# Four gate projections of z brought forward into the first four rounds of a chunked delta rule

## The reference

```
h = rms_norm(x);  proj = h @ w_in      # glu_a glu_b q k v z a b gate_a gate_b
c = silu(layer_norm(conv31(glu_a * sigmoid(glu_b))));  y_conv = c @ w_conv_out
q, k, v = silu(conv5(q, k, v)); q, k normed per head (8 heads of 128)
o = delta_rule(q, k, v, g, beta) + reversed delta_rule   # chunks along the sequence
o = rms_norm(o) * silu(z);             y_delta = o @ w_delta_out
x = x + (sigmoid(gate_a) * y_conv + sigmoid(gate_b) * y_delta) @ w_o
```

## Time and profile before

| | |
|---|---|
| median of three runs | 2165.98 us (2165.07 to 2167.03) |
| profiled execution, its time | 2168.76 us |
| profiled execution, its span | 2167.0 us |
| mean granted TensorE clock | 0.995 |
| PE, DVE, ACT, POOL busy | 2105.1, 1210.3, 853.3, 154.5 us |
| rounds 0 to 3 | 216.2 to 412.3 us of the span |
| rounds 4 to 7 | 499.1 to 696.0 us |

### The profile page before, as it was taken

How to read it: one execution, slowest core, us unless ns; L and a number is a source line. 1 busy time by engine, 2 the same in 40 slices (tenths; PEclk the granted TensorE clock), 3 DMA queues, 4 the chain that set the end, 5 groups by cost and what they waited for, 6 DMA issues and landing times.

```text
span 2167.0 us, 35176 instructions
## 1 busy us (share of the span) xinstructions
PE 2105.1 (97%) x14346; PEld 1747.7 (81%) x14346; DVE 1210.3 (56%) x1888; ACT 853.3 (39%) x1400; POOL 154.5 (7%) x134
## 2 busy tenths in 40 slices
PE   6999999999999999999999999999999999999998
PEld 5878777787878888888888888888897688888887
DVE  4789888798645554444433644443247835444323
ACT  4344655346674333333223533332243544322222
POOL 0100021002421010000000100000000110000000
PEclk9999999999999999999999999999999999999999
DMA  4242111122012342233323233233212122333321
GB/s 166 81 134 80 60 46 50 60 78 65 31 63 87 127 159 88 97 97 97 120 94 107 69 90 96 96 101 111 98 59 62 37 69 79 96 96 97 116 94 53
DMA packets 56173, 189.95 MB, mean 88 GB/s; under 512 B 6256, under 2 KB 8688, under 8 KB 56048
## 3 DMA queue, kind: packets, MB, share of 16 engines
q1 hardware_dynamic: 53168, 182.92, 26.4%
q10 hardware_dynamic: 2880, 5.24, 0.6%
HBM read 178.70 MB, written 9.44 MB: 87 GB/s over the span
## 4 chain that ended last, share of the span: by engine, by line
PE 65%; DVE 3%; ACT 1%; issue 0%; POOL 0%; DVEq 0%; ACTq 0%
PE pg L716 61%; PE pC L820 1%; DVE w_lo L2021 1%; PE pA L794 0%; PE pC L794 0%; PE pB L778 0%; ACT w_hi L1393 0%; PE pB L747 0%; DVE a_lo L2080 0%; DVE sml L2680 0%; DVE sm L2678 0%; PE pA L754 0%; DVE mo L2717 0%; PE pC L1308 0%; ACT a_hi L1953 0%
## 5 line engine op out<-in xcount | busy, mean ns | idle before, releaser
L716 PE MATMUL pg<-a_hi,w_hi 128*128 128x512 f32 (+1 forms) x1920 | 747.4, 389 | 14.2 <-ACT ptile L1483 4.4
L716 PE MATMUL pg<-a_lo,w_hi 128*128 128x512 f32 (+1 forms) x1920 | 739.9, 385 | 0.0
L716 PE MATMUL pg<-a_hi,w_lo 128*128 128x512 f32 (+1 forms) x1920 | 737.9, 384 | 0.0
L2021 DVE TENSOR_TENSOR w_lo<-w_raw,w_hi 128x1024 fp32r<-128x1024 f32 (+3 forms) x299 | 386.3, 1292 | 386.7 <-ACT w_hi L1393 386.0
L1393 ACT ACTIVATE w_hi<-w_raw 128x1024 fp32r<-128x1024 f32 (+3 forms) x299 | 329.6, 1102 | 646.0 <-PE pg L716 635.4
L716 PEld LDWEIGHTS pg<-a_hi,w_hi 128*128 128x128 f32 x1920 | 362.3, 189 | 91.3 <-issue 9.2
L716 PEld LDWEIGHTS pg<-a_hi,w_lo 128*128 128x128 f32 x1920 | 361.9, 188 | 68.9 <-issue 1.4
L716 PEld LDWEIGHTS pg<-a_lo,w_hi 128*128 128x128 f32 x1920 | 362.3, 189 | 67.8 <-issue 0.9
L716 PE MATMUL pg<-h_hi,w_hi 128*128 128x512 f32 (+1 forms) x572 | 213.5, 373 | 0.5 <-DVE w_lo L2021 0.5
L716 PE MATMUL pg<-h_hi,w_lo 128*128 128x512 f32 (+1 forms) x572 | 213.3, 373 | 0.0
L716 PE MATMUL pg<-h_lo,w_hi 128*128 128x512 f32 (+1 forms) x572 | 213.2, 373 | 0.0
(11 more groups left out here) (397 smaller groups left out, 2216.7 us busy)
## 6 DMA issues: line engine op xcount, KB each, us to landing
w_raw<-in_w_gu SPq DMA_DIRECT2D x132, 512.0 KB, 3.5
w_raw<-in_w_in SPq DMA_DIRECT2D x74, 512.0 KB, 3.5
w_raw<-in_w_dn SPq DMA_DIRECT2D x48, 704.0 KB, 4.1
spill_g<-tmp ACTq DMA_DIRECT2D x16, 256.0 KB, 2.2
w_raw<-in_w_co SPq DMA_DIRECT2D x8, 512.0 KB, 3.9
w_raw<-in_w_do SPq DMA_DIRECT2D x8, 512.0 KB, 3.7
w_raw<-in_w_wo SPq DMA_DIRECT2D x8, 512.0 KB, 4.2
w_raw<-in_w_pg SPq DMA_DIRECT2D x8, 512.0 KB, 3.5
```

What stands on the lines that cost most here:

```text
L716: ins = pe.matmul(dst[:, cols], w_of(w, n % 2, k), b(k)[:, cols], start=first and q == 0, stop=last and q == len(todo) - 1)
L2021: dve.tensor_tensor(w_lo[:, n % 2, 0:c], w_raw[:, n % 4, 0:c], w_hi[:, n % 2, 0:c].bitcast(F32), ALU.subtract).then_inc(S("w_lo"), 1)
```

## The change

Rounds 0 to 3 get a fourth filler, z4 to z7. Round 4 keeps gates 14 and 15, round 5 gets z0 and z1, round 6 gets z2 and z3; these three now have two fillers each and are dealt out by a new list `GAP2`. Round 7 keeps its four. The order of units and banks follows. Rounds 0 to 3 now use `GAP` and get 12 taps instead of 10 at gap 14; round 4 gets 16 taps instead of 24. Some waits for spills are counted anew, and SP waits for `on_z` before it loads the first two gates back.

```diff
+        FILLERS = [[("gate", 3 * R + 1), ("gate", 3 * R + 2), ("gate", 3 * R + 3), ("z", HH + R)] for R in range(4)] + [
+            [("gate", 14), ("gate", 15)], [("z", 0), ("z", 1)], [("z", 2), ("z", 3)], [("co", f) for f in range(4)]]
...
         GAP = [16, 17, 4, A_, B_, A_, B_, 1, B_] + [A_, B_] * 2 + [6, 8, 8]
-        GAP3 = [14, 14, 2, 3, 3, 3, 3, 1, 3] + [3, 3] * 2 + [4, 5, 5]
-        TAP = [1, 2, 0] + [1, 2] * 2 + [1, 3, 1, 2, 1, 3] + [0, 10, 0]
-        TAP4 = [1, 2, 0] + [1, 1] * 4 + [1, 2] + [0, 10, 0]
+        GAP2 = [9, 9, 4, 2, 2, 2, 2, 1, 2, 2, 2, 2, 2, 2, 2, 3]
+        TAP = [1, 2, 0] + [1, 2] * 2 + [1, 3, 1, 2, 1, 3] + [0, 12, 0]
+        TAP4 = [1, 1, 0] + [1, 1] * 5 + [0, 4, 0]
...
-        FILLERS = [[("gate", 3 * R + f) for f in range(1, 4)] for R in range(4)] + [
-            [("gate", 14), ("gate", 15), ("z", 0)], [("z", f) for f in range(1, 4)],
-            [("z", f) for f in range(4, 8)], [("co", f) for f in range(4)]]
...
-            gaps = GAP3 if len(filler(R)) == 3 else GAP
+            gaps = {2: GAP2, 4: GAP}[len(filler(R))]
...
                         if t < 2:
                             sp.wait_ge(S(f"spill{t}"), 16 * 10)
+                            sp.wait_ge(S("on_z"), 3 + t)
...
-                elif k in (13, 14):
+                elif k in (17, 18):
                     act.wait_ge(S("ons"), HH)
-                elif k < 18:
+                elif k < 22:
                     act.wait_ge(S(f"spill{k % 2}"), 16 * (k // 2))
-                elif k < 22:
-                    act.wait_ge(S("on_z"), k - 17)
                 else:
-                    act.wait_ge(S(f"spill{k % 2}"), 16 * (k // 2 - 2))
+                    act.wait_ge(S("on_z"), k - 21)
```

More of the change, by code:

```diff
@@ L323, in qkv_units, with filler_units @@
                     U.add(("qkv", 3 * h + i), a["w_in"][(2 + i) * KT + h], KT * P)
+        FILLERS = [[("gate", 3 * R + 1), ("gate", 3 * R + 2), ("gate", 3 * R + 3), ("z", HH + R)] for R in range(4)] + [
+            [("gate", 14), ("gate", 15)], [("z", 0), ("z", 1)], [("z", 2), ("z", 3)], [("co", f) for f in range(4)]]
+        TAIL = (("gate", 0), ("gate", 13))
+        def filler_units(half):
+            for key in [TAIL[half]] + sum(FILLERS[NC * half:NC * half + 4 - half], []):
+                U.add(key, a["w_in"][{"gate": 6, "z": 5}[key[0]] * KT + key[1]], KT * P)
         qkv_units(0)
-        for i in range(13):
-            U.add(("gate", i), a["w_in"][6 * KT + i], KT * P)
+        filler_units(0)
         qkv_units(1)
[L329 to L332, removed]
+        filler_units(1)
         for nm in ("co", "do", "wo"):
@@ L380, in build @@
         O.add(("ab",), "D")
-        TAIL = (("gate", 0), ("gate", 13))
         def qkv_outs(half):
@@ L389, in qkv_outs @@
             O.add(TAIL[half], "A")
[L391 to L398, removed]
+        for half in range(2):
+            qkv_outs(half)
+            for key in sum(FILLERS[NC * half:NC * half + 4 - half], []):
+                O.add(key, "A")
         for i in range(8):
@@ L484, in build @@
         UNIT = 3 * KT
-        assert sum(GAP) == 4 * UNIT and sum(GAP3) == 3 * UNIT and \
+        assert sum(GAP) == 4 * UNIT and sum(GAP2) == 2 * UNIT and \
             4 * GLU_TAPS[0] + 6 * GLU_TAPS[1] + sum(sum(z) for q in QKV_TAPS for z in q) + 4 * sum(TAP) + sum(TAP4) >= len(TAPS)
@@ L1583, in head_squares @@
                         if g < 2:
-                            act.wait_ge(S(f"spill{g}"), 16 * (7 - g))
+                            act.wait_ge(S(f"spill{g}"), 16 * (9 - g))
                         else:
```

## The result

The changed kernel takes 2187.18 us (median of 3, 2185.73 to 2187.54) against 2165.98, and the ratio on record is 1.0085 with a 95% interval of 1.0071 to 1.0099. By these medians it is slower by 21 us (a quotient of 1.0098), where I had said 8. The ratio fits about 2168.5 us for the kernel before, and that is also the mean of its 91 executions further down; by it the loss is 18 us. The profiled execution took 2185.73 us. Lines in a row are those of the kernel it comes from: 984, 1002, 1039, 1112, 1129 and 1718 of the changed kernel are 989, 1007, 1044, 1117, 1134 and 1725 before, and 1002, 1020, 1130, 1147 and 1737 in the version with two units moved are 989, 1007, 1117, 1134 and 1725 before.

What follows compares the result with a forecast made beforehand. PE was taken as dense nearly throughout, with DVE setting the pace in rounds 0 to 3. Terms +7.3 and -4.7 gave +2.6, plus +5 for clock falls: 2176.4 us profiled, about 2174 median, range 2161 to 2183.

Steps and rivals of the forecast that it cites:

- Round 0, +6.4: Round 0 with a fourth filler: 2.7 us stall for yb in level 3 and a longer DVE-set tail, +6.4 us.
- Rounds 1 to 3, +2.8, -0.6, -1.3: Fourth filler partly hidden; rounds 2 and 3 each regain 3.4 us as their old clock falls go.
- The table load that the last silu brings: End of rounds 0 to 2: one more ACT table load, 1.28 us, hidden in 2 us of slack.
- Rounds 4 to 6, structure -4.7: Rounds with two fillers, tied by ACT or POOL steps: +0.6, +0.5 and -5.8 us, sum -4.7.
- the term of the clock: Emptier rounds 4 to 6, and round 0: two to three clock falls of 2 to 3 us each, +5 us.
- B: Clock stays low through rounds 4 to 6, over half of about 140 us: 12 to 15 us, about 2183; chance 0.12.
- A: Fillers of rounds 0 to 3 hide in ub waits, falls go, rounds 5 and 6 shrink: about 2159 us; chance 0.15.
- C: No new clock falls, the two old ones go, only structure counts: 2169 us; chance 0.23.
- D: The old clock falls stay in rounds 2 and 3 as well: 2180 us; chance 0.08.
- The taps: Round 0 to 3 tails: 12 taps of about 0.67 us, 8.0 us, before oT; round 4 has eight taps less.

Runs made afterwards that it cites:

- the version with two units moved: Against the kernel before, only two units of z moved, to rounds 2 and 3 (fillers 3, 3, 4, 4, 3, 3, 2), taps as before: ratio 1.0009.
- the version with 24 products ahead: Against the changed kernel, rounds with two fillers put 24 instead of 18 products ahead of the levels: 2173.88 us, ratio 1.0025 to the kernel before.
- the run with filled waits: Changed kernel plus 63 products of no use in nine PE waits of rounds 0, 4, 5 and 6: 2178.40 us, ratio 1.0046 to the kernel before.
- the version with two moved and the gate output behind `yb`: Two units moved, with round 6's gate table and gate output put behind yb and kt of level 2: ratio 1.0006 to the kernel before.

## Why the prediction was wrong

**Round 0, +6.4: right.** Measured +7.7 with one fall in it. Line 1002 of level 3 waits for `yb` by 2.15 us (2.7 forecast). The tail, from line 1112 to the next round, is 14.2 us long (254.97 to 269.20), as forecast, and the two rows of DVE above show its cause: `w_lo`, the taps and `oT` set its end. What the forecast lacks lies ahead of line 1112 and is the fall: from level 0 to there the round takes 25.4 us (229.56 to 254.97), and 23.9 (229.72 to 253.66) in the version with 24 products ahead, whose round 0 has the same instructions and a clock of 1.00:

```profile
213.90:267.90 54.00, 47.68 (x736) 37.71 (x735) 44.85 (x85) 34.00 (x67) 4.56 (x7) 1.00 0.23 73
```

**Rounds 1 to 3, +2.8, -0.6, -1.3: right,** +2.6, -0.6 and -1.6. Both old falls are gone, and the waits at line 1112 with them, 0.2 us in rounds 1 and 2. The table load that the last silu brings cost nothing, as forecast: no wait at the head of these rounds is for ACT.

```profile
PE pC L1002 <- ACT yb L1718: 1.6, 2, 0.8
PE pA L1039 <- DVE oT L2417: 1.5, 1, 1.5
...
PE pC L1112 <- DVE ub L2378: 0.2, 1, 0.2
```

**Rounds 4 to 6, structure -4.7: right in its mechanism and nearly in size.** The wait of 4.3 us for POOL and the late `yb` of level 2 are in the rows above. The tail of round 6 is 2.0 us shorter up to line 1129 (2.4 forecast), though its wait for `en`, which I said would go, is still 2.0 us. Round 5 with the clock at 1.00 took 48.7 us and round 6 50.5 (waits filled), against my 48 and 51. Round 4 I had at 45; with its 18 products ahead it was never seen at full clock, and 49.2 us with 10.2 at half clock is the nearest.

**The failing step is the term of the clock.** I wrote "two to three falls, each 2 to 3 us", +5 in all, reasoning from the falls of round 2, which last 7 us. There were five low stretches in rounds 0 to 6, and the one of round 4 lasted over 20 us without a break. Lengths less the structural forecast leave 1.3, 9.0, 3.1 and 1.3 us for rounds 0, 4, 5 and 6, so 14.7. That it is all clock is shown for round 0 by the 1.5 us above and borne out for rounds 5 and 6 by the run with filled waits; for round 4 it is argued: at the prices of 0.28 to 0.39 us for each us at half clock (last section), the 37.5 us of rounds 4 to 6 cost 10.5 to 14.6, an estimate, and 13.4 are to be explained. For the profiled execution I had 2176.4 us; with 14.7 for 5 it is 2186.1, and it measured 2185.73. The median is off by 3.5 us more: I took 2.8 off because the median of three lay that far below the profiled execution, but over 91 runs the kernel before has a median of 2168.12 us, so the three were fast ones.

What I overlooked is that a fall among sparse levels can last. In round 4 each step waits for the next engine, PE offers little work whatever its clock, and only the dense tail of the round brought 1.00 back. It isn't a rule: the other four stretches, the first of round 4 among them, ended after 3.4 to 6.8 us. But every profile of a round 4 with 18 products ahead has 10 us or more at half clock in one stretch. Level 4, from its `yb` to the next, took 5.2 us (538.96 to 544.18) against 3.8 in the version with 24 products ahead (534.45 to 538.26), itself at 0.60 for the first part of that time:

```profile
538.96 0.60 ACT L1718 ACTIVATE yb<-pC 128x512 f32<-128x512 f32 x1 [4.26 <-PE pC L984]
544.18 0.60 ACT L1718 ACTIVATE yb<-pC 128x512 f32<-128x512 f32 x1 [4.63 <-PE pC L984]
```

```profile
534.45 0.60 ACT L1718 ACTIVATE yb<-pC 128x512 f32<-128x512 f32 x1 [3.17 <-PE pC L984]
538.26 0.60 ACT L1718 ACTIVATE yb<-pC 128x512 f32<-128x512 f32 x1 [3.21 <-PE pC L984]
```

**The rivals.** B had the right mechanism and, at 2183 us, nearly the right size, but not its place: 37.5 us of rounds 4 to 6 were at half clock, not 70, and 20 of them lie in one stretch. I gave it 0.12 because round 4 had idled 3.2 us at clock 1.00. But in that round the waits for POOL and `yb` were 1.78 and 1.16 us, 10 us apart; the change makes them 4.3 and 1.8 us, 8 us apart. A is wrong (round 5 took 51.6 us, and 48.7 without its low clock, over the 46 at which it decides), C and D too.

**The taps** I did price in round 0, rightly as the rows show, and counted as less work in round 4. That they cost 0.2 to 0.3% by themselves, mostly through a lower mean clock, was in no term. It may be part of the 14.7 and is not to be added to it.

What stays open: why a fall comes at one place in one execution and not in the next. The 91 runs of the kernel before range from 2163.6 to 2175.0 us with nothing changed. Nor was it tried how round 4 runs with its POOL wait taken away at the root.

## What to carry over

When work is moved out of a stretch, look at what its products covered, and price the clock by how long PE stays sparse behind a wait, not by the falls seen in fuller stretches. In a thin stretch the gap in which a unit ends matters: five products put later moved copy, table load and output of another engine ahead of a value that the chain waited for, left another gap empty, and cost 0.3%. And a forecast of a few us needs several executions of the kernel before, with their clocks: here 0.001 of mean clock is 1.5 us.

## What the runs showed of the hardware

**The price of the low clock.** Over the 91 runs of the kernel before, 0.001 of mean clock is 4.3 us at 1.2 GHz (2 x 0.001 x 2167) and costs 1.53 us, 0.35 us for each. Round 4 gives 0.28 (54.0 to 49.2 us for 27.3 to 10.2 us at half clock), round 6 of the version with two moved 0.39 (56.4 to 51.1 us for 13.6). A fuller stretch gives more: round 1 with three fillers takes 48.3 us at clock 1.00, and 51.4 in a run that has the same instructions there and 6.9 us at half clock, 0.45 for each. The Trainium skill (TensorE: Matmul & The Clock Gate, HAM oscillation — how this bites in real kernels) counts half of the time spent throttled as lost. By that, the 27.3 us of round 4 would have cost an estimated 13.6, and the residual was 9.0. The fuller round comes near the page's half, and the rounds in which PE waits for other engines stay below it.

**Products of no use are not free** even where PE waits: nine fillings put the mean clock back to 0.995 and left the kernel 11 us slower than the kernel before at that clock. Part of that is the changed kernel's own 7 us.

**Falls change place by themselves.** Filling the wait of round 4 shortened it by 4.8 us, and round 6 was 3.8 us longer, in a stretch whose instructions were the same. Whether the filling did that isn't shown. In the version with two moved and the gate output behind `yb`, round 1 has clocks of 0.92, 0.50 and 0.72 in three rows of 4 us from 296 us; in the profile of the version that it differs from only in round 6, round 1 has 1.00 throughout.
